# Modulation products of a two-part block: from matmuls on TensorE to multiplies with a row sum on VectorE

## The reference, cut to what matters

```
x = first_block(x, mem, ...)      # norm, local attention + mLSTM, w_out; cross attention; gated FFN; final norm
c_act = silu(c)                   # c: one row of 1024
for layer in (0, 1):
    mod = c_act @ w_ada[layer] + b_ada[layer]          # 1024 x 3072
    shift, scale, gate = mod[:, :D], mod[:, D:2*D], mod[:, 2*D:]
    h = rms(x) * g * (1 + scale) + shift
    layer 0: y = gated delta rule over h (qkv with a 4-tap convolution, z gate) @ w_out
    layer 1: mkv = c_act @ w_ada_kv + b_ada_kv         # 1024 x 2048, modulates the norm in front of k and v
             y = stick-breaking attention @ w_out
    x = x + gate * y
```

## Time and profile before

| | |
|---|---|
| median of 3 runs | 977.05 us (975.28 to 979.23) |
| the profiled execution's own time | 978.81 us |
| its span, first to last instruction | 976.8 us |
| mean granted PE clock | 0.952 of full speed |
| PE busy | 903.1 us, 92% |
| DVE busy | 577.8 us, 59% |
| ACT busy | 503.6 us, 52% |
| DMA | 148.09 MB, mean 152 GB/s |

### The profile page before, as it was taken

How to read it: one execution, slowest core, us unless ns; L and a number is a source line. 1 busy time by engine, 2 the same in 40 slices (tenths; PEclk the granted TensorE clock), 3 DMA queues, 4 the chain that set the end, 5 groups by cost and what they waited for, 6 DMA issues and landing times.

```text
span 976.8 us, 18099 instructions
## 1 busy us (share of the span) xinstructions
PE 903.1 (92%) x7690; PEld 822.9 (84%) x7690; DVE 577.8 (59%) x1203; ACT 503.6 (52%) x1031; POOL 0.5 (0%) x5
## 2 busy tenths in 40 slices
PE   3998999999999999999969899989897979999998
PEld 3977898989899999999968687869696968888888
DVE  5277556574667777765656665565554556533354
ACT  5365553454445555545554725352744467356762
POOL 0000000000000000000000000000000000000000
PEclk9999899999999999999987998989998979999999
DMA  9323443653355676646552333223322233641211
GB/s 350 136 88 122 177 169 129 240 193 129 129 179 216 254 255 226 227 188 208 192 216 87 135 128 137 77 93 125 99 76 87 87 130 130 261 149 66 87 44 44
DMA packets 22544, 148.09 MB, mean 152 GB/s; under 512 B 2624, under 2 KB 3008, under 8 KB 6336
## 3 DMA queue, kind: packets, MB, share of 16 engines
q1 hardware_dynamic: 22464, 146.94, 41.1%
HBM read 145.88 MB, written 1.05 MB: 150 GB/s over the span
## 4 chain that ended last, share of the span: by engine, by line
PE 81%; DVE 10%; ACT 7%; issue 1%; DMA 1%; SPq 0%; DVEq 0%; ACTq 0%
PE ps L1872 57%; PE ps L1885 3%; DVE wlo L1398 2%; PE ps L2104 1%; PE ps L1893 1%; DVE kT L1395 1%; PE ps L1922 1%; ACT L1009 1%; PE ps L2194 1%; PE ps L2114 1%; DVE vt L1395 1%; ACT tmp L1083 1%; PE ps L2086 1%; PE ps L2185 1%; PE ps L2045 1%
## 5 line engine op out<-in xcount | busy, mean ns | idle before, releaser
L1872 PE MATMUL ps<-p0hi,whi 128*128 128x256 f32 x1128 | 339.8, 301 | 17.1 <-DVE p0lo L1398 12.5
L1872 PE MATMUL ps<-p0lo,whi 128*128 128x256 f32 x1128 | 326.1, 289 | 0.0
L1872 PE MATMUL ps<-p0hi,wlo 128*128 128x256 f32 x1128 | 325.7, 289 | 0.0
L1398 DVE TENSOR_TENSOR wlo<-raw,whi 128x512 fp32r<-128x512 f32 (+2 forms) x436 | 273.0, 660 | 22.8 <-ACT whi L1029 21.4
L1872 PEld LDWEIGHTS ps<-p0hi,whi 128*128 128x128 f32 x1128 | 222.8, 197 | 34.6 <-issue 22.7
L1029 ACT ACTIVATE whi<-raw 128x512 fp32r<-128x512 f32 (+2 forms) x436 | 239.6, 599 | 7.5 <-DMA raw<-wst 5.8
L1872 PEld LDWEIGHTS ps<-p0lo,whi 128*128 128x128 f32 x1128 | 223.4, 198 | 0.7 <-issue 0.5
L1872 PEld LDWEIGHTS ps<-p0hi,wlo 128*128 128x128 f32 x1128 | 223.2, 198 | 0.0
L1872 PE MATMUL ps<-zhi,whi 128*128 128x256 f32 x176 | 49.3, 280 | 0.0
L1872 PE MATMUL ps<-zlo,whi 128*128 128x256 f32 x176 | 49.3, 280 | 0.0
L1872 PE MATMUL ps<-zhi,wlo 128*128 128x256 f32 x176 | 49.1, 279 | 0.0
(11 more groups left out here) (347 smaller groups left out, 1517.7 us busy)
## 6 DMA issues: line engine op xcount, KB each, us to landing
raw<-wst SPq DMA_DIRECT2D x125, 1024.0 KB, 4.8
raw<-wsd SPq DMA_DIRECT2D x16, 704.0 KB, 4.2
x<-xT SPq DMA_DIRECT2D x4, 256.0 KB, 5.0
m_x<-memT SPq DMA_DIRECT2D x1, 1024.0 KB, 17.5
outT<-x SPq DMA_DIRECT2D x4, 256.0 KB, 2.0
cst<-con SPq DMA_DIRECT2D x1, 416.0 KB, 12.4
smo<-conr SPq DMA_DIRECT2D x1, 320.0 KB, 11.8
vc<-vec SPq DMA_DIRECT2D x1, 187.5 KB, 2.5
```

What stands on the lines that cost most here:

```text
L1398: return v.tensor_tensor(lo, src, hi.bitcast(F32), ALU.subtract)
L1872: ins = t.matmul(o, a, b, start=first and q == 0, stop=last and q == len(ops) - 1, skip_group_check=True)
```

## The change

The 32 products move from PE to DVE. The weights of the three modulation matrices are laid out transposed in memory: a unit holds two blocks of 128 output columns, with the outputs on partitions and 1024 inputs along the row. c is loaded repeated on all 128 partitions (0.5 MB, issued ahead of unit 7), and its silu is taken on ACT over 128x1024, after the silus of the first convolution. A new job `ada` on DVE does two `tensor_tensor_reduce` instructions for a unit: multiply by c_act, write the products over the weights in `raw`, and sum them, starting from the bias, into one column of `mod`. The jobs `adarow`, `adacp`, `adacol`, `adaadd`, the late list of the plan, the tile `arow` and the zeroing of `cact` on POOL are gone. The load of unit k+5 behind a modulation unit k now waits for DVE's `ada`.

The modulation units stand in other places of the order: none before `xk`, then 9 up to `xo` (behind `xk` 1 and 3, `xv` 0, `wout` 1 and 3, `xv` 2, `xq` 1 and 3, `xo` 1), 8 in `up` (11 before), 3 in `down` (none before), 4 in `qkva` (behind every third unit; 8 before), 2 in `za`, 2 in `outa`, 4 in `sbv` as before.

In the first stage ACT loads the table for logarithm and exponential at once and makes no silu first; and the groups of normed chunks take turns with the quarters of the first weight unit (group, quarter, group ...) in place of the unit first.

```diff
     add("aq", 0, 2)
     add("akv", 0)
-    mixed("mqk", 0, 4, 2)
-    mixed("mv", 0, 2, 2)
+    add("mqk", 0, 4)
+    add("mv", 0, 2)
     add("mo", 0, 2)
-    mixed("xk", 0, 4, 2)
-    add("xv", 0)
-    mixed("wout", 0, 4, 2)
-    add("xv", 1, 2)
-    add("xq", 0, 4)
+    mixed("xk", 0, 4, (1, 3))
+    mixed("xv", 0, 1, (0,))
+    mixed("wout", 0, 4, (1, 3))
+    mixed("xv", 1, 2, (2,))
+    mixed("xq", 0, 4, (1, 3))
     add("xv", 3)
-    mixed("xo", 0, 4, 2)
-    mixed("up", 0, 22, 2)
-    add("down", 0, 16, 11, 128)
+    mixed("xo", 0, 4, (1,))
+    mixed("up", 0, 22, (1, 4, 7, 10, 13, 16, 18, 20))
+    for i in range(16):
+        add("down", i, 1, 11, 128)
+        if i in (3, 7, 11):
+            add(*ada.pop(0))
     for i in range(4):
         for part in range(3):
             add("qkva", 4 * part + i)
-            if part != 1:
-                add(*ada.pop(0))
-    add("za", 0, 4)
-    add("outa", 0, 4)
+        add(*ada.pop(0))
+    mixed("za", 0, 4, (1, 3))
+    mixed("outa", 0, 4, (1, 3))
     add("sbk", 0, 4)
-    mixed("sbv", 0, 4, 1)
+    mixed("sbv", 0, 4, (0, 1, 2, 3))
...
     def ada_part(self):
         k = self.carried.pop(0)
-        self.run_late(True)
-        self.add("adarow", k)
-        self.add("adacp", k)
+        self.add("ada", k)
         self.loaded_free.add(k)
         self.load_units()
-        self.late.append([3, k])
...
     def make(self):
-        add("csilu", "c")
...
         self.load_units()
-        for _ in range(PIECES):
-            self.prep_unit()
-        for _ in self.gain_steps("mix"):
-            pass
+        add("xg", "mix", 0)
+        for i in range(len(GROUPS)):
+            if i != 1:
+                self.prep_unit()
+                self.flush_lows()
+            self.split_group("mix", i)
+            if i + 1 < len(GROUPS):
+                add("xg", "mix", i + 1)
         add("cr")
...
                 if k >= NRAW:
                     if is_ada(units[k - NRAW]):
-                        e.wait_ge(*on("adarow", k - NRAW))
+                        e.wait_ge(*on("ada", k - NRAW))
...
-            e.wait_ge(*landed("vec"))
-            e.wait_ge(zeroed, 1)
-            silu(cact[:, :, 0], V("c", 0, 8)).then_inc(*tick("csilu"))
+            lnexp()
...
-                elif kind == "adaadd":
-                    name, n = i
+                elif kind == "ada":
+                    k, = i
+                    name, n = units[k][:2]
                     col, bname = {"ada0": (0, "b_ada0"), "ada1": (24, "b_ada1"), "adakv": (48, "b_kv")}[name]
-                    e.wait_ge(*on("adacol", at(name, n)))
-                    v.tensor_tensor(mod[...], stats[:, T:T + 2], V(bname, 2 * n, 2), ALU.add).then_inc(*tick("adaadd"))
+                    e.wait_ge(*arrived(k))
+                    e.wait_ge(*on("csilu", "c"))
+                    e.wait_ge(*landed("vec"))
+                    for m in range(2):
+                        r = raw[k % NRAW][:, m * D:(m + 1) * D]
+                        c = col + 2 * n + m
+                        ins = v.tensor_tensor_reduce(out=r, in0=r, in1=cact[:, :], scale=1.0, scalar=V(bname, 2 * n + m), op0=ALU.mult,
+                                                     op1=ALU.add, accum_out=mod[:, c:c + 1])
+                    ins.then_inc(*tick("ada"))
...
-                elif kind == "adarow":
...
-                    for c in range(KC):
-                        g = 32 * (c % 4)
-                        ins = t.matmul(stats[g:g + 32, T:2 * T], cact[:, c, :], r[:, c * T:(c + 1) * T], start=c < 4, stop=c >= 4)
-                elif kind == "adacol":
...
-                    for m in range(2):
-                        ins = t.matmul(stats[:, T + m:T + m + 1], arow[:, m * P:(m + 1) * P], ones[:, 0:1], start=True, stop=True)
```

More of the change, by code:

```diff
@@ L118, in unit_order, with mixed @@
     ada = [("ada0", i) for i in range(12)] + [("adakv", i) for i in range(8)] + [("ada1", i) for i in range(12)]
-    def mixed(name, first, n, every):
+    def mixed(name, first, n, places):
         for i in range(first, first + n):
             add(name, i)
-            if every and i % every == every - 1:
+            if i in places:
                 add(*ada.pop(0))
@@ L161 @@
 COUNTED = {
-    "hi": "hi", "lo": "lo", "unit": "unit", "adarow": "adarow", "adacp": "adacp", "adacol": "adacol",
-    "adaadd": "adaadd",
+    "hi": "hi", "lo": "lo", "unit": "unit", "ada": "ada",
     "sq": "sq", "sqadd": "sqadd", "ones": "ones", "mones": "ones", "rs": "rs",
@@ L208, in __init__ @@
         self.slot_free = [True] * NHL
-        self.lows, self.deferred, self.carried, self.late = [], [], [], []
+        self.lows, self.deferred, self.carried = [], [], []
         self.done = set()
@@ L397, in rest @@
                 if i == 3:
-                    self.deferred.extend([lambda n=n: add("csilu", n) for n in range(4)])
+                    self.deferred.extend([lambda n=n: add("csilu", n) for n in range(4)] + [lambda: add("csilu", "c")])
             later(rest)
@@ L766, in wait_ge, with program @@
             self.seen[sem.name] = n
-def program(nc, xT, memT, vec, con, conr, wg1, wg2, wst, wsd, outT):
+def program(nc, xT, memT, cB, vec, con, conr, wg1, wg2, wst, wsd, outT):
     plan = Plan().make()
@@ L789, in program @@
         s_raw = [sem(f"s_raw{i}") for i in range(NRAW)]
-        s_in = {n: sem("s_in_" + n) for n in ("x0", "x1", "x2", "x3", "mem", "vec", "con", "con2", "conr", "g")}
+        s_in = {n: sem("s_in_" + n) for n in ("x0", "x1", "x2", "x3", "mem", "vec", "con", "con2", "conr", "g", "c")}
         s_out = sem("s_out")
-        own_act, own_dve, zeroed = sem("s_own_act"), sem("s_own_dve"), sem("s_zeroed")
+        own_act, own_dve = sem("s_own_act"), sem("s_own_dve")
         def on(*job):
@@ L824, in program @@
         g2 = sb("g2", [P, KC, 16])
-        cact = sb("cact", [P, KC, 32])
+        cact = sb("cact", [P, D])
         mod = sb("mod", [P, 64])
@@ L980, in _ @@
                     load("mem", m_x[:, :, :], memT)
+                if k == 7:
+                    load("c", cact[:, :], cB)
                 if kc == 8:
@@ L1029, in _ @@
                     act.activation(whi[n % NHL][:, a:b], raw[k % NRAW][:, a:b], ACT.Copy).then_inc(*tick("hi"))
[L1030 to L1033, removed]
                 elif kind == "sq":
@@ L1107, in _ @@
                     ins.then_inc(*tick("cid"))
-                elif kind == "csilu" and i != ["c"]:
+                elif kind == "csilu" and i == ["c"]:
+                    e.wait_ge(*landed("c"))
+                    silu(cact[:, :], cact[:, :]).then_inc(*tick("csilu"))
+                elif kind == "csilu":
                     n, = i
@@ L1513, in _ @@
                     if name == "outa":
-                        e.wait_ge(*on("adaadd", "ada0", 11))
+                        e.wait_ge(*on("ada", at("ada0", 11)))
                         for m in range(2):
@@ L1524, in _ @@
                     e.wait_ge(*unit_done("outb", n))
-                    e.wait_ge(*on("adaadd", "ada1", 11))
+                    e.wait_ge(*on("ada", at("ada1", 11)))
                     for m in range(2):
@@ L1568, in _ @@
                     col, gain, last = {"a": (8, "g_a", ("ada0", 7)), "kv": (56, "g_kv", ("adakv", 7)), "b": (32, "g_b", ("ada1", 7))}[site]
-                    e.wait_ge(*on("adaadd", *last))
+                    e.wait_ge(*on("ada", at(*last)))
                     m = mod[:, col:col + 8]
@@ L2256 @@
     put("q_gain", np.tile(f["q_gain_b_2"].reshape(64, 1), (2, 1)))
-    put("c", colsof(f["c_2"], 8))
     put("sink", np.repeat(f["attn_sinks"].reshape(1, 8), P, 0))
@@ L2280 @@
     laid = {n: unit_layout(w, 11 if n == "down" else 8, 128 if n == "down" else 256) for n, w in mats.items()}
+    for n in ("ada0", "ada1", "adakv"):
+        laid[n] = np.ascontiguousarray(mats[n].T).reshape(-1, 2, P, D).transpose(0, 2, 1, 3).reshape(-1, P * 2048)
     order = unit_order()
```

22 lines of the change are left out of this document (2 added, 20 removed).

## The result

| | median us (range, runs) | ratio to before (95%) | profiled span |
|---|---|---|---|
| before | 977.1 (975.28 to 979.23, 4) | 1 | 976.8 |
| after | 964.73 (960.83 to 968.6, 4) | 0.9873 [0.9826, 0.9919] | 964.2 |

The changed kernel is 1.3% faster (95% interval 0.8% to 1.7%, clear of no change): 12.4 us, where 17 were forecast (960, range 943 to 975).

The account below looks back on a forecast made before the run. PE was taken as the bound (92% busy, 81% of the chain). Gain 40.0 + 2.3 = 42.3 less DVE cost 25.6 gave net 16.7: 978.81 to 962.1 us, 960 in the median, range 943 to 975.

Parts of the forecast that it names:

- The gain, 40.0 us for the modulation's lines: PE path: removing the row product and its turning into columns, 4.1% of the chain, saves 40.0 us.
- The instruction, 1.3 us: Each new 128x1024 f32 instruction with running sum on DVE takes 1.3 us, 2.6 us a unit.
- The slow rival: DVE at two cycles an element: a unit costs 5.0 us, total 1013 us in the median; chance 0.12.
- First stage, 2.3 us: Start of the kernel: earlier table load and one weight quarter ahead let PE start sooner, gaining 2.3 us (0 to 3.5).
- 45 to 283 us, 5.6 us: Stretch from 45 to 283 us: nine modulation units on DVE cost 5.6 us together.
- `up`, 7 us: `up`: DVE's later low parts exceed a slack of 0.8 us and make PE wait, costing 7 us (3 to 9.3).
- `down`, nothing: `down`: three units cost nothing, as DVE has no taps and no silu to follow there.
- Delta rule, 11.5 us: Delta rule: six units cost 11.5 us (5 to 16), mostly three ahead of the mask at 3.0 each.
- Point 4: Expected sign: the delta stage stays as long as before within 4 us.
- 762 to 977, 1.5 us: Stretch from 762 to 977 us: two units in `outa` and four in `sbv` cost 1.5 us for both.
- Points 1 and 2: Expected signs: new instruction 1.2 to 1.45 us, DVE busy about 655 us; PE busy about 855 to 870, lines 1885 and 1893 gone.
- Point 3: Expected sign: an `up` pair takes 12.3 to 12.6 us instead of 13.12, with small waits of PE for `wlo`.

Follow-up runs that it names:

- thin: Changed kernel with both instructions of each modulation unit working on 2 elements instead of 1024; 924.71 us, ratio 0.949 to the kernel before.

## Why the prediction was right, and where its terms were off

The direction, the mechanism in the main (PE's time won, a part of it lost where DVE's next result is what PE waits for) and the time (960 against 964.73) held. But both terms of the sum were too small, by 8 and by 11 us, and made up for each other: that the forecast came within 5 us is in part luck. By the ratios the freed PE time is what thin shows, 0.051 x 977 = 50 us where I credited 42.3, and the cost on DVE is 37 us where I charged 25.6.

- *The gain, 40.0 us for the modulation's lines: undersized.* I took the chain's share of lines 1885 and 1893. The matmuls beside them were slowed, too. In the earlier trace rows 36 large matmuls between the row product and the columns take 4.50 us, 125 ns each, and 60 take 7.29, 121.5 each; in `down` of the same kernel, without modulation, the chain has one long piece:

```profile
442.39 59.13 PE ps L1872 x501
```

  That is 118.0 ns each. The time line of PE at a row product (start, length) has the reason:

```profile
306.12 0.28 PE L1872 MATMUL ps<-p0hi,wlo 128*128 128x256 f32 x1
306.33 1.07 PE L1885 MATMUL ps<-raw,cact 128*32 128x256 f32 x16
307.33 0.39 PE L1872 MATMUL ps<-p0hi,whi 128*128 128x256 f32 x1
307.55 0.28 PE L1872 MATMUL ps<-p0lo,whi 128*128 128x256 f32 x1
307.67 0.28 PE L1872 MATMUL ps<-p0hi,wlo 128*128 128x256 f32 x1
```

  Around the row product the step is 0.21 and 0.22 us instead of 0.12: each change between the two kinds of matmul costs the neighbour 0.1 us, which the chain books as the neighbour's. A pair of `up` units needs 2 x 5.68 us (48 matmuls of 118.3 ns in thin), so a modulation unit took 13.12 - 11.36 = 1.76 us of PE, not 1.34. For 32 units that is 56 us if all were on the path; 50 came out.
- *The instruction, 1.3 us: right.* 1.28, at a pitch of 1.20, where the bounds were 1.2 and 2.5. The read-out of the sum takes 0.01 us in the chain. By the records with 2 elements (216 ns) and with 1024 (1280) an element costs 1.04 ns, the slope of the plain two-source instruction. The slow rival (chance 0.12) is out. The half-rate rule of the Trainium skill (Vector Engine (DVE) Microarchitecture Reference, 7. Points that are easy to get wrong), which the page states for scalar_tensor_tensor, does not hold for this instruction: 1024 f32 elements with two SBUF sources and an accumulator output take 1.17 ns an element by the pitch.
- *First stage, 2.3 us: not seen.* PE started at 15.10 us (point 5 said near 14.5), with x landed at 8.77 instead of 7.57 in that profile. It did 12 matmuls at the slow step of 0.21 us, then stood idle for 0.58 us:

```profile
15.10 0.55 PE L1866 MATMUL ps<-p0hi,whi 128*128 128x256 f32 x1 [2.68 <-DVE p0lo L1383]
...
18.59 0.55 PE L1866 MATMUL ps<-p0hi,whi 128*128 128x256 f32 x1 [0.58 <-DVE p0lo L1383]
```

  The turns bring nothing that can be told (ratio 0.9868 with the old order). What the table's 1.28 us bring was not tried by itself; in the profile of that kernel and of this one it is within the scatter of the stretch.
- *45 to 283 us, 5.6 us: right in kind, low.* After minus thin is 8.3 us in the two stretches, 5.7 of them for the two units of `xq`, which I had put at 1 and 2.6 us.
- *`up`, 7 us: the step that failed is PE's need.* Against 5.89 us a unit I found a slack of 0.8 us a turn for DVE to use up; PE's need without the modulation was 5.68, and DVE's turn of 5.33 left 0.35. From the norm sum ahead of it to `down`'s first long piece after takes 137.7 us (291.62 to 429.36); thin, up to the same matmul, takes 127.9 (278.29 to 406.21): a cost of 10 us. The net gain of `up` (from the norm sum to `down`'s first matmul 132.7 us instead of 143.1) was still larger than forecast, 11 x 1.34 - 7 = 7.7, as the neighbours' time came with it.
- *`down`, nothing: wrong, 4.8 us.* I looked at DVE's load (it has no taps there) and not at what stands ahead of the unit in DVE's order. The load was not the matter: 7 units fit at even places, and only an eighth cost 1.0 us.
- *Delta rule, 11.5 us: right.* 13.4 - 0.3 us measured, by the mechanism foretold: at 577, 629 and 679 us the chain has the mask right behind a unit. Point 4, as long as before within 4 us, holds: 3.6 longer in the long stretch.
- *762 to 977, 1.5 us: right.* 1.6 in `outa`, nothing in `sbv`.
- Points 1 and 2 held but for DVE busy 647.7 us instead of 655, of which the new instruction is 3.5 (79.5 us for the 83 foretold); PE's 856.8 lies in 855 to 870. Point 3 (a pair of 12.3 to 12.6 us) missed by 0.12: DVE sets this period, with a turn of 5.3 and a unit of 2.4 where I had 5.37 and 2.6.

## What to carry to other kernels

A share of the chain by line understates what a foreign kind of matmul costs: take a stretch of the same work without it and compare the time per matmul. Work moved to a second engine is paid in full where that engine sets the pace (`up`, 2.4 us a unit). Elsewhere it is paid by its place in that engine's queue and not by the engine's load: here 2.4 us of VectorE cost nothing (`sbv`, `down` behind an even unit), 1.6 (behind a residual that waits for TensorE) or 3 (in a recurrence, mostly ahead of a mask), and moving the same 32 units to the free places gained twice as much again as the change itself. To size such a cost, run the kernel with the new work cut to two elements and, if it may hurt, doubled.

## What was not expected of the hardware

- Matmuls of two shapes in turn cost PE 0.1 us at each change (steps of 0.21 and 0.22 us for 0.12).
- A multiply with a running row sum in f32 (1.28 us for 1024 elements) has the slope of the plain two-source instruction (1.04 ns an element, by the records with 2 and with 1024 elements), and a row reduction of 1024 takes 1.21 us.
- After PE had stood idle for 3.7 us the granted clock was 0.66 in the next 4 us; after 1.5 us, the same 99 matmuls ran at full speed. The doubled work cost 87 us for 77 us of VectorE, the single one 37 for 68 (79.5 us less the 11.4 that the instructions on 2 elements still took).
- The same code took 69.1 to 75.2 us for the first stretch in ten profiles; the granted clock from 38 to 73 us was 0.90 and 0.76 at the two ends.
